# Two activation buffers that begin 12 bytes into a 64-byte line

## The chip, the cores and the metric

The kernel runs on one core of a Trainium2 chip. The metric is the time of one execution on the device in microseconds: 2912.06 us, the median of 3 runs (2911.98 to 2912.39).

## The reference

Two transformer-like blocks are computed one after the other for one sequence of 512 tokens with 1024 features, in float32. Nearly all the work is in dense products of a normalised activation with a weight matrix:

```python
# first block
n = rmsnorm(h, norm_mix_g[l]);  proj = (n @ w_in[l])
y_rwkv = rwkv7_mix(...)         # a recurrent scan over 16 heads, in chunks of 64 tokens
y_attn = dilated_mixture(...)   # 12 heads of windowed attention
merged = sigmoid(gate_r) * (y_rwkv @ p_rwkv) + sigmoid(gate_a) * (y_attn @ p_attn)
h = h + merged @ w_out
h = h + memory_cross_attention(rmsnorm(h), rmsnorm(mem), xa_wq, xa_wkv, xa_wo)
h = h + square(relu(rmsnorm(h) @ ffn_w1)) @ ffn_w2
# second block, two layers
h = rmsnorm_2(x) * (1 + sc1) + sh1
x = x + g1 * token_mix(h, ...)  # fourier_mix and a retention branch, both gated
h = rmsnorm_2(x) * (1 + sc2) + sh2
x = x + g2 * conv_ffn(h, w_up, conv_w, conv_b, w_down)
```

## The kernel before

**Products.** TensorE multiplies float32r operands. To keep float32 accuracy, every operand is split into a high part (rounded to float32r) and a low part (the rest), and each 128 x 128 block of weights gives three matmuls: weight high by activation high, weight high by activation low, weight low by activation high. In `tile` these are L906, L907 and L910. There the weight block is the stationary operand, which is loaded first (PEld in the profile), and a row of the activation with 512 columns (256 for a half tile) is the moving operand, which streams through. Where the output is wanted with tokens on the partitions, the roles are exchanged (L899 to L901): a 128-column piece of the activation is stationary and the weights move.

**Buffers.** Weights come by DMA as units of 128 x 1024 into w_raw (3 slots). ScalarE casts a unit into w_hi (L1862), and GpSimd writes the difference into w_lo (L837, in quarters); w_hi and w_lo have 5 slots. Activations lie in act2 (called A2) and act1 (A1). Each has, on every partition, 2 parts (high, low) of 8 rows of 512 elements of 4 bytes. ScalarE writes a high row (`high`, L1889), VectorE the low row as the difference (`low`, L2600). Smaller buffers follow: act_attn, params, table, tmp, squares, and a large one, arena, which holds nearly all else; arena_r is the same memory as arena seen as float32r, and arena2 is the same memory as act2 seen as float32, used as scratch in the first stages.

**Where they start.** Buffers are laid one behind the other in the order of the program, each rounded up to 32 bytes. From the sizes: w_raw begins at byte 1152 of each partition, w_hi at 13440, w_lo at 33920, act2 at 54400, act1 at 87168, act_attn at 119936, table at 130720, tmp at 137152, squares (and squares_r) at 141248, arena at 148384. Modulo 64 these are 0 for the w and act buffers, tmp and squares, and 32 for table and arena. Rows of act1 and act2 are 2048 bytes apart, so each of them begins at 0 modulo 64. A view in the arena begins wherever the sizes ahead of it put it: `spectrum`, the moving operand of `fourier_tile` (L958 to L960), is at element 16491 of the arena. `folded_tile` (L934 to L936) does the same kind of product from act2. In retention (L1770 to L1772, L1784 to L1786) both operands are data: RK, RQ, RV and RP, whose high parts lie in act_attn, squares_r and act2 and whose low parts lie in the arena.

**Order.** Each engine runs its own list of instructions, fixed when the program is built; they meet at semaphores. The table of tiles (`make_plan`) sets TensorE's order, and four banks of the accumulator are used in turn for them. Nothing in it depends on addresses.

Of the kernel before, what the change touches and what calls it, by code (L numbers as in the profile page):

```python
# [16 lines left out]
P = 128  # L17
F32 = mybir.dt.float32
F32R = mybir.dt.float32r
# [5 lines left out]
S = 512  # L25
M = 256
KT = D // P
# [8 lines left out]
LAYERS = 2  # L36
RING, RAWS = 5, 3
AHEAD = 3
TAIL, W2 = 4, S // 2
BANKS = 4  # L40
ARENA = 20128
# [229 lines left out]
def build_program(nc, plan, ap, out):  # L271
# [19 lines left out]
    with ctx:  # L291
        def sb(name, shape, dt=F32):
            return ctx.enter_context(nc.sbuf_tensor(name, shape, dt))
# [3 lines left out]
        def sem(name):  # L297
            if name not in sems:
                sems[name] = ctx.enter_context(nc.semaphore(name))
            return sems[name]  # L300
# [3 lines left out]
        w_lo = sb("w_lo", [P, RING, UNIT], F32R)  # L304


        with nc.sbuf_tensor("arena2", [P, 2 * KT * S], F32) as arena2:
            pass
        acts = {"A2": sb("act2", [P, 2, KT, S], F32R), "A1": sb("act1", [P, 2, KT, S], F32R)}
        with nc.sbuf_tensor("relu", [P, 2, S], F32) as RELU:  # L310
            pass
        acts["YA"] = sb("act_attn", [P, 2, 2, S], F32R)
# [432 lines left out]
        def half_requests(name):  # L745

            t = stages[CLOSED[name]][1] - 1
            n = TC if name == "final" else TC // 2
            return [(t, n, spare_slots(name)), (t, n, 3)] if name != "out" else [(t, n, 0)] * 2
# [16 lines left out]
        for l in range(LAYERS):  # L766
            if l:
                REQUESTS += half_requests(f"n1_{l}")
            for hd in range(XH):
                before = f"ret_k{l}_{hd + 1}" if hd + 1 < XH else f"ret_g{l}_{hd}"  # L770
                REQUESTS += [(stages[before][1] - 1, TC, AHEAD + (hd + 1 == XH))]
            REQUESTS += half_requests(f"n2_{l}")
# [45 lines left out]
        def _(pool):  # L818
            done = [0]

            def low_weights(end):
                for u in range(done[0], min(end, n_units)):
                    if u in BY_VECTOR:
                        continue
                    k = u % RING
                    pool.wait_ge(sem("w_high" if u else "first_high"), u + 1)
                    if u >= RING:
                        unit_free(pool, u - RING)
                    if u in MIDDLE_UNITS:
                        nc.gpsimd.tensor_tensor(middle_columns(w_lo[:, k, :]), middle_columns(w_raw[:, u % RAWS, :]),  # L830
                                                middle_columns(w_hi[:, k, :].bitcast(F32)), ALU.subtract).then_inc(sem("w_low"), 1)
                        continue
                    for c in range(0, UNIT, UNIT // 4):
                        if u == 0 and c == UNIT // 2:
                            pool.wait_ge(sem("w_high"), 1)
                        cols = slice(c, c + UNIT // 4)
                        ins = nc.gpsimd.tensor_tensor(w_lo[:, k, cols], weights_of(u)[:, cols], w_hi[:, k, cols].bitcast(F32),  # L837
                                                      ALU.subtract)
                        if u < 2 and c < UNIT - UNIT // 4:
                            ins.then_inc(sem("first_low"), 1)  # L840
                    ins.then_inc(sem("w_low"), 1)
                done[0] = max(done[0], min(end, n_units))
# [5 lines left out]
            for r, (t, cols, *ahead) in enumerate(REQUESTS):  # L848
                ahead = ahead[0] if ahead else AHEAD
                low_weights(max(u for u, _, _ in tiles[t]["blocks"]) + 1 + ahead if t is not None else AHEAD)  # L850
                pool.wait_ge(sem("stats_ready"), r + 1)
# [2917 lines left out]
```

## Time and profile before

| | |
|---|---|
| median of 3 runs | 2912.06 us |
| span of the profiled execution | 2909.9 us |
| its own time beside the span | the runs shown lie about 2.2 us above the span |
| PE (matmuls) busy | 2892.3 us, 99% of the span |
| PEld (loads of stationary operands) busy | 2423.8 us, 83% |
| POOL busy | 1584.3 us, 54% |
| DVE busy | 1572.7 us, 54% |
| ACT busy | 1103.5 us, 38% |
| DMA | 322 MB, mean 111 GB/s |

PE is TensorE's matmuls, DVE is VectorE, ACT is ScalarE, POOL is GpSimd. A matmul's duration in the profile runs from its start to its modelled end, and the next one starts before that end, so that durations overlap and a busy share of 99% says only that there is hardly a gap. What a matmul costs in a row of them is the distance from its start to the next one's start, which the list of instructions in order of time gives.

### The profile page before, as it was taken

The page shows a single profiled execution, that of the slowest core. Times are in us where ns is not written, and L with a number is a line of the kernel's source. Part 1 is how long each engine was busy: PE and PEld are TensorE (multiplying, and loading weights), DVE is VectorE, ACT ScalarE, POOL GpSimd, SP SyncE. Part 2 cuts the span into 40 slices and gives each one's busy share as a digit, 9 for nine tenths or more (in the row PEclk, how much of TensorE's full clock was granted, in tenths as well). Part 3 has the DMA queues.
Part 4 walks back from the last instruction along what each step waited for, and adds up shares of the span by engine and source line. Part 5 has one row for each costly group of instructions (what it writes and reads, how often), then busy time and mean ns, then how long its engine had stood idle before and what let it go on. Part 6 is the DMA issues. An engine that isn't in the chain of part 4 may idle for free.

```text
span 2909.9 us, 49401 instructions
## 1 busy us (share of the span) xinstructions
PE 2892.3 (99%) x19658; PEld 2423.8 (83%) x19658; DVE 1572.7 (54%) x2227; ACT 1103.5 (38%) x1673; POOL 1584.3 (54%) x1912
## 2 busy tenths in 40 slices
PE   9999999999999999999999999999999999999998
PEld 7877777788888888888888898888898888988887
DVE  5467877524556666775334265445763441473635
ACT  4454434333443322443433343233443342342323
POOL 6432233355646666677444557565584444565654
PEclk9999999999999999999999999999999999999999
DMA  5211111332426777533222323232333222232232
GB/s 173 94 45 41 42 55 45 97 141 95 130 82 217 252 273 254 179 113 126 85 89 73 95 87 113 87 109 87 106 124 115 77 88 87 87 102 94 94 102 73
DMA packets 92292, 322.21 MB, mean 111 GB/s; under 512 B 10144, under 2 KB 14368, under 8 KB 91808
## 3 DMA queue, kind: packets, MB, share of 16 engines
q1 hardware_dynamic: 84544, 302.39, 31.7%
q10 hardware_dynamic: 7520, 16.67, 1.7%
q8 instruction: 156, 2.56, 0.4%
q14 instruction: 72, 0.59, 0.1%
HBM read 315.09 MB, written 3.93 MB: 110 GB/s over the span
## 4 chain that ended last, share of the span: by engine, by line
PE 98%; issue 1%; DVE 1%; POOL 1%; DMA 0%; ACT 0%; POOLq 0%; SPq 0%; ACTq 0%; DVEq 0%
PE bank L906 25%; PE bank L910 25%; PE bank L907 25%; PE bank L1254 2%; PE bank L899 2%; PE bank L901 2%; PE bank L900 2%; PE bank L1265 2%; PE bank L1273 1%; PE bank L934 1%; PE bank L936 1%; PE bank L935 1%; PE bank L958 1%; PE bank L960 1%; PE bank L1785 1%
## 5 line engine op out<-in xcount | busy, mean ns | idle before, releaser
L837 POOL TENSOR_TENSOR w_lo<-w_raw,w_hi 128x256 fp32r<-128x256 f32 x1736 | 1419.2, 852 | 986.9 <-ACT w_hi L1862 980.5
L906 PE MATMUL bank<-act,w_hi 128*128 128x512 f32 (+1 forms) x3464 | 1312.7, 379 | 4.7 <-POOL w_lo L837 2.6
L910 PE MATMUL bank<-act,w_lo 128*128 128x512 f32 (+1 forms) x3464 | 1292.4, 373 | 0.0
L907 PE MATMUL bank<-act,w_hi 128*128 128x512 f32 (+1 forms) x3464 | 1291.4, 373 | 0.0
L906 PEld LDWEIGHTS bank<-act,w_hi 128*128 128x128 f32 x3464 | 652.9, 188 | 126.1 <-issue 8.3
L910 PEld LDWEIGHTS bank<-act,w_lo 128*128 128x128 f32 x3464 | 652.6, 188 | 115.2
L907 PEld LDWEIGHTS bank<-act,w_hi 128*128 128x128 f32 x3464 | 653.4, 189 | 106.7
L1862 ACT CAST w_hi<-w_raw 128x1024 fp32r<-128x1024 f32 (+1 forms) x438 | 454.4, 1043 | 345.1 <-DMA w_raw<-in_weights 163.6
L1870 ACT ACTIVATE arena<-bank 128x512 f32<-128x512 f32 (+1 forms) x177 | 104.3, 593 | 418.2 <-PE bank L910 401.6
L855 POOL TENSOR_TENSOR stats<-stats,exponent 128x8 f32<-128x8 f32 (+2 forms) x38 | 46.6, 1226 | 302.5 <-DVE stats L2914 150.0
L2600 DVE TENSOR_TENSOR act<-tmp,act 128x512 fp32r<-128x512 f32 (+1 forms) x140 | 121.2, 866 | 77.3 <-ACT act L1889 72.7
L3588 DVE TENSOR_SCALAR arena<-arena,params 128x512 f32<-128x512 f32 x88 | 53.0, 602 | 172.3 <-ACT arena L1870 171.9
L3323 DVE SCALAR_TENSOR_TENSOR arena<-arena,small 128x1024 f32<-128x1024 f32 x93 | 136.5, 1468 | 3.3
L837 POOL TENSOR_TENSOR w_lo<-arena,w_hi 128x256 fp32r<-128x256 f32 x128 | 114.9, 932 | 22.5 <-ACT w_hi L1862 22.5
L1889 ACT CAST act<-tmp 128x512 fp32r<-128x512 f32 (+1 forms) x140 | 84.4, 605 | 112.5 <-DVE tmp L3212 32.0
L2773 DVE SCALAR_TENSOR_TENSOR arena<-bank,small,arena 128x512 f32<-128x512 f32 x48 | 36.1, 751 | 166.9 <-PE bank L910 166.6
L2125 ACT ACTIVATE arena<-bank 128x512 f32<-128x512 f32 (+1 forms) x104 | 64.8, 631 | 114.3 <-PE bank L1273 96.9
L899 PE MATMUL bank<-w_hi,act 128*128 128x512 f32 (+1 forms) x224 | 84.5, 377 | 0.0
L3591 DVE SCALAR_TENSOR_TENSOR arena<-arena,params 128x512 f32<-128x512 f32 x88 | 82.6, 939 | 3.1
L901 PE MATMUL bank<-w_hi,act 128*128 128x512 f32 (+1 forms) x224 | 83.7, 374 | 0.0
L900 PE MATMUL bank<-w_lo,act 128*128 128x512 f32 (+1 forms) x224 | 83.7, 374 | 0.0
L2771 DVE TENSOR_TENSOR arena<-arena,bank 128x512 f32<-128x512 f32 x44 | 30.3, 688 | 89.5 <-PE bank L910 89.2
(359 smaller groups left out, 3087.4 us busy)
## 6 DMA issues: line engine op xcount, KB each, us to landing
w_raw<-in_weights SPq DMA_DIRECT2D x471, 512.0 KB, 3.5
arena<-in_ada SPq DMA_DIRECT2D x96, 512.0 KB, 5.0
arena<-in_strips ACTq DMA_DIRECT2D x8, 448.0 KB, 3.7
arena<-in_x ACTq DMA_DIRECT2D x1, 2048.0 KB, 10.9
y_scratch<-tmp ACTq DMA_DIRECT2D x7, 256.0 KB, 2.0
arena<-y_scratch ACTq DMA_DIRECT2D x1, 1792.0 KB, 8.1
arena<-in_dft ACTq DMA_DIRECT2D x2, 777.5 KB, 4.2
arena<-in_x SPq DMA_DIRECT2D x3, 512.0 KB, 7.4
```

The lines of the kernel that those rows point to most:

```text
L837: ins = nc.gpsimd.tensor_tensor(w_lo[:, k, cols], weights_of(u)[:, cols], w_hi[:, k, cols].bitcast(F32), ALU.subtract)
L899: nc.tensor.matmul(o, xs[0], wh, start=first, stop=False)
L900: nc.tensor.matmul(o, xs[0], wl, start=False, stop=False)
L901: mm = nc.tensor.matmul(o, xs[1], wh, start=False, stop=last)
L906: nc.tensor.matmul(o, wh, xh, start=first, stop=False)
L907: nc.tensor.matmul(o, wh, xl, start=False, stop=False)
L910: mm = nc.tensor.matmul(o, wl, xh, start=False, stop=last)
L1862: nc.scalar.copy(x, y).then_inc(sem("w_high"), 1)
L1870: nc.scalar.activation(dst, banks[bank_of(t)][:, 0:n], func, scale=scale).then_inc(sem(f"bank_free{bank_of(t)}"), 1)
L1889: ins = nc.scalar.copy(o, x) if shift is None else nc.scalar.activation(o, x, ACT.Identity, bias=shift)
L2600: do(V_.tensor_tensor(o, x, h, ALU.subtract), "low_done")
L3323: do(V_.scalar_tensor_tensor(o, w, c_act[:, k:k + 1], o, ALU.mult, ALU.add), "ada_used")
```

## The change

act2, act1 and arena2 get 16 elements (64 bytes) more per partition, and the part that is used begins 3 elements (12 bytes) into them. The rows within a buffer stay 2048 bytes apart. The sub-views are made from the shifted views, so all users follow. act1 begins 64 bytes later than before, everything behind act1 128 bytes later.

```diff
+LINE, LINE_AT = 16, 3
...
-        with nc.sbuf_tensor("arena2", [P, 2 * KT * S], F32) as arena2:
-            pass
-        acts = {"A2": sb("act2", [P, 2, KT, S], F32R), "A1": sb("act1", [P, 2, KT, S], F32R)}
+        with nc.sbuf_tensor("arena2", [P, 2 * KT * S + LINE], F32) as arena2:
+            arena2 = arena2[:, LINE_AT:LINE_AT + 2 * KT * S]
+        acts = {name: sb(buf, [P, 2 * KT * S + LINE], F32R)[:, LINE_AT:LINE_AT + 2 * KT * S].rearrange(
+            "p (a k s) -> p a k s", a=2, s=S) for name, buf in (("A2", "act2"), ("A1", "act1"))}
```

The program has the same 26400 instructions in the same order with the same waits, and the same lengths of their operands; only start addresses differ. Source lines behind the change are 2 higher (L906, L907, L910 become L908, L909, L912).

## Rows read from the trace of the kernel before

**Rows 1.** The page: busy time, and the chain that ended last.
```profile
PE 2892.3 (99%) x19658; PEld 2423.8 (83%) x19658; DVE 1572.7 (54%) x2227; ACT 1103.5 (38%) x1673; POOL 1584.3 (54%) x1912
...
PE 98%; issue 1%; DVE 1%; POOL 1%; DMA 0%; ACT 0%; POOLq 0%; SPq 0%; ACTq 0%; DVEq 0%
```
**Rows 2.** Waits of TensorE: waiter, releaser, us in total, times, longest.
```profile
PE bank L906 <- POOL w_lo L837: 2.6, 2, 2.3
...
PE bank L1312 <- PE bank L1301: 0.2, 1, 0.2
```
**Rows 3.** TensorE's groups by shape: count, busy us and mean ns, idle before.
```profile
L906 PE MATMUL bank<-act,w_hi 128*128 128x512 f32 x2920 | 1156.5, 396 | 2.4 <-POOL w_lo L837 2.3
L910 PE MATMUL bank<-act,w_lo 128*128 128x512 f32 x2920 | 1138.7, 390 | 0.0
L907 PE MATMUL bank<-act,w_hi 128*128 128x512 f32 x2920 | 1137.6, 390 | 0.0
L906 PE MATMUL bank<-act,w_hi 128*128 128x256 f32 x544 | 156.2, 287 | 2.3 <-DVE act L2602 1.0 <-DVE arena L2700 0.8 <-POOL w_lo L837 0.4
...
L899 PE MATMUL bank<-w_hi,act 128*128 128x512 f32 x160 | 62.4, 390 | 0.0
...
L899 PE MATMUL bank<-w_hi,act 128*128 128x384 f32 x64 | 22.0, 344 | 0.0
```
**Rows 4.** In order of time, a long stage: start us, us, instruction.
```profile
1453.28 0.39 PE L910 MATMUL bank<-act,w_lo 128*128 128x512 f32 x1
...
1455.55 0.39 PE L906 MATMUL bank<-act,w_hi 128*128 128x512 f32 x1
```
**Rows 5.** VectorE's groups by shape: two sources on 4-byte words, one shape.
```profile
L2600 DVE TENSOR_TENSOR act<-tmp,act 128x512 fp32r<-128x512 f32 x132 | 116.6, 884 | 76.9 <-ACT act L1889 72.7
...
L2821 DVE TENSOR_TENSOR square_sum<-arena 128x512 f32<-128x512 f32 x27 | 18.9, 701 | 0.9
...
L2600 DVE TENSOR_TENSOR act<-arena,act 128x512 fp32r<-128x512 f32 x16 | 13.7, 857 | 15.3 <-ACT act L1889 15.0
...
L3561 DVE TENSOR_TENSOR arena<-arena 128x512 f32<-128x512 f32 x16 | 11.1, 692 | 0.6
...
L3427 DVE TENSOR_TENSOR arena_r<-bank,arena_r 128x512 fp32r<-128x512 f32 x8 | 5.5, 692 | 16.8 <-ACT arena_r L2385 16.7
```
**Rows 6.** ScalarE's groups by shape: casts.
```profile
L1862 ACT CAST w_hi<-w_raw 128x1024 fp32r<-128x1024 f32 x436 | 453.9, 1047 | 345.1 <-DMA w_raw<-in_weights 163.6 <-PE bank L910 105.3 <-DVE arena L3205 58.7
...
L1862 ACT CAST w_hi<-arena 128x1024 fp32r<-128x1024 f32 x32 | 33.5, 1048 | 32.4 <-DVE arena L3407 19.8 <-DVE arena L3397 12.5
...
L2385 ACT CAST arena_r<-bank 128x512 fp32r<-128x512 f32 x8 | 4.7, 584 | 7.1 <-PE bank L1718 7.1
L2304 ACT CAST act_attn<-bank 128x512 fp32r<-128x512 f32 x8 | 4.3, 590 | 2.8 <-PE bank L1617 2.8
```
**Rows 7.** In order of time, 256 columns from act2 (folded_tile), 14 distances.
```profile
1285.30 0.28 PE L934 MATMUL bank<-act,w_hi 128*128 128x256 f32 x1
...
1286.98 0.28 PE L936 MATMUL bank<-act,w_lo 128*128 128x256 f32 x1
```
**Rows 8.** In order of time, after small matmuls: 7 distances, then 8.
```profile
75.95 0.39 PE L907 MATMUL bank<-act,w_hi 128*128 128x512 f32 x1
...
77.56 0.39 PE L910 MATMUL bank<-act,w_lo 128*128 128x512 f32 x1
...
79.38 0.39 PE L907 MATMUL bank<-act,w_hi 128*128 128x512 f32 x1
```
**Rows 9.** In order of time, retention, 12 distances.
```profile
1418.51 0.40 PE L1784 MATMUL bank<-act,squares_r 128*128 128x512 f32 x1
1418.74 0.40 PE L1785 MATMUL bank<-arena_r,squares_r 128*128 128x512 f32 x1
1418.98 0.40 PE L1786 MATMUL bank<-act,arena_r 128*128 128x512 f32 x1
...
1421.31 0.40 PE L1784 MATMUL bank<-act,squares_r 128*128 128x512 f32 x1
```
**Rows 10.** In order of time, fourier_tile, 18 distances.
```profile
1318.88 0.28 PE L958 MATMUL bank<-arena_r,w_hi 128*128 128x256 f32 x1
...
1321.00 0.28 PE L958 MATMUL bank<-arena_r,w_hi 128*128 128x256 f32 x1
```
**Rows 11.** Stretches: span, busy us and count of each engine, PEclk (granted), DMA.
```profile
1850.00:1950.00 100.00, 100.00 (x443) 82.81 (x442) 51.86 (x64) 34.91 (x49) 67.74 (x80) 1.00 0.32 103
```
**Rows 12.** TensorE's groups by shape between 200 and 560 us.
```profile
L906 PE MATMUL bank<-act,w_hi 128*128 128x512 f32 x209 | 95.6, 457 | 0.0
```

## The prediction

> **What bounds the kernel now.** I read the page's chain of waits first. It gives 98% of the span to TensorE [rows 1], and the list of waits shows under 10 us in which TensorE stood still for another engine, the largest single entry 2.6 us [rows 2]. The reader is to see two things: the end is set by how closely TensorE's matmuls follow each other, and VectorE, ScalarE and GpSimd (54%, 38%, 54% busy) would have to get much slower before they mattered. The second view is the groups by shape [rows 3]: 3 x 2920 matmuls of 512 columns read an activation buffer as the moving operand and a weight slice as the stationary one; 3 x 544 do so with 256 columns; 672 (3 x 160 and 3 x 64) have the roles exchanged. The durations in these rows overlap, so they are not the price. The price is the distance from start to start, read in the third view, the instructions in order of time: in a long stage ten distances take 2.27 us, 227 ns each [rows 4]. 8760 of them make 1989 us, 68% of the span. All depends on whether this 227 moves.
>
> **The change part by part.** No instruction is added, removed or moved; only start addresses differ. w_raw, w_hi and w_lo stay. act2 and act1 each get 64 bytes more, so everything behind them moves by 64 or 128 bytes and keeps its place in a 64-byte line. What changes is every operand in act2, act1 and arena2 (an alias of act2): it begins 12 bytes into a line, an odd 4-byte word.
>
> First, the engines that write and read these buffers. The kernel already has such operands. VectorE's L2821 subtracts two rows of RAW that lie one word apart, so one of them starts on an odd word: 701 ns, against 692 for L3561, whose sources both start 32 bytes into a line. L3427 reads and writes `spectrum`, which lies 12 bytes into a line (148384 + 4 x 16491 bytes; that is 12 modulo 64): 692 ns [rows 5]. ScalarE's cast needs 1048 ns from the odd words of the arena and 1047 from w_raw; its cast into `spectrum` 584, into the aligned act_attn 590 [rows 6]. GpSimd's w_lo touches no moved buffer. So the price here is 0 by the nearest rows. From above I take 9 ns (701 - 692) on the 148 subtractions of L2600 [rows 5] and twice as many others, 4 us, and all of it lies under TensorE, which waits for other engines under 10 us in all. From below it is no gain either. I take 0.
>
> The Trainium skill speaks against the change here: "Vector Engine (DVE) Microarchitecture Reference", section 5.2, says that a port runs at full rate only in runs of adjacent words that start on an 8-byte boundary, and gives 1.30 instead of 1.054 ns per column for pairs on an odd word. By it L2821 and L3427 ought to take over 100 ns more than their neighbours; they don't, so for one long run the trace does not bear it out. Even with it the sum stays, since VectorE is covered.
>
> Second, TensorE's reads. The distance is regular to a degree that tells something: 227 ns for 512 columns, 120 for 256 [rows 4, 7], both 13.3 ns above columns/2.4 GHz; the granted clock is 1.00 in the long stage, the upper of its two levels, 2.4 GHz [rows 11]. But this is a state into which the stream settles. After a few small fp32 matmuls seven distances take 1.61 us, 230 ns each, and the next eight 1.82 us, 227.5 [rows 8]; same operands, same addresses. In retention, 512-column matmuls in which some operands lie 32 bytes into a line (arena) and others 0 (act2, squares_r, act_attn) never settle: twelve distances take 2.80 us, 233.3 ns each, with single ones between 230 and 240 [rows 9]. They are long runs with weights ready, so nothing is waited for. For 256 columns it is the other way round: in fourier_tile the moving operand is `spectrum`, 12 bytes into a line, with the stationary one on a line start from w_hi or w_lo. That is exactly the pairing which the change makes. Eighteen distances (half of 258 columns, half of 256) take 2.12 us, 117.8 ns each, 2.2 below the settled 120 [rows 10]. So 12 bytes do not cost a 256-column matmul anything; they do keep it from the settled rhythm. My reading is that the unsettled rhythm is worth -2 ns at 256 columns and +3 to +7 at 512.
>
> No row shows 512 columns at 12 bytes. The bounds of its price: from below -2.2 ns (rows 10, a gain by instruction), from above +10 (a distance of 237, about the longest that repeats in rows 9). Nearest in length and in steadiness is the retention pattern, +6.6; the settling runs give +3. I take +6.
>
> The sum: of the 8760, some 626 stand in the scan between 200 and 560 us in groups of three to six between small matmuls (209 for L906) [rows 12] and have not settled today, so they cost the same. 8134 x 6 ns = 48.8 us. The 672 with exchanged roles, whose stationary operand now starts at 12 bytes, at the same price: 4.0 us. 1632 of 256 columns x -2.2 ns = -3.6 us. Together +49.2 us. The fp32 matmuls of the scan that read arena2 have their own rhythm and short runs: 0. All of TensorE's time is on the path, so it goes straight to the end: 2909.9 + 49.2 = 2959.1 us of span. The median of the runs shown, 2912.06, lies 2.2 above the span of the profiled execution, which gives 2961.
>
> The Trainium skill, "TensorE: Matmul & The Clock Gate", section "Wait — 56ns, not 53.3ns?", puts back-to-back matmuls at columns/2.4 GHz plus about 2.5 ns, with no word on addresses. By it a 512-column one would follow after 216 ns; the trace has 227, so 11 ns here are something that the page does not know. If they came from two reads that start alike, and the 12 bytes parted them, the sum would be negative: that is case (b) below, driven further.
>
> **The rivals.**
> (a) The rhythm settles again, since all moving operands shift by the same 12 bytes and the weights by none: every matmul meets the next under the same condition, only at another phase. For it: 256 columns settle just as 512 do [rows 7], and settling takes but seven matmuls [rows 8]. Against it: fourier_tile has just such uniform offsets over groups of 24 and does not come to 120. Time: 2912, within 0.2%.
> (b) The other side, faster: what the 12 bytes do at 256 columns they do at 512, because the surplus belongs to the instruction (one weight load) and not to the columns. Price -2.2 ns x (8134 + 672 + 1632) = -23 us: 2889. For it: rows 10 are the only rows with the very pairing. Against it: rows 9, where 512 columns off the settled rhythm are always slower than 227, and rows 8. It decides from the point where the mean distance of L906 falls below 226.7.
> (c) VectorE suffers after all: a quarter more on L2600's 117 us [rows 5] is 29 us, and as much again on the rest. Nearly all of it is hidden under TensorE; if the waits of rows 2 doubled, it would be +10 us, 2922 alone.
> (d) The change doesn't do what it says: act2 and act1 could be placed so that the offset is undone. The kernel's sizes give 54400 + 12 and 87232 + 12, both 12 modulo 64, so no.
>
> **How the numbers follow.** A run of this kernel can be told from another at about 0.2%, 5.8 us. The unsettled rhythm has 0.44 (2961, its own range 2930 to 2998, from +2.5 to +10 ns), the settled one 0.24 (2912), the gain 0.29 (2889, down to 2870), VectorE's part alone 0.03, half of it over the limit. Slower (by over 5.8 us) is thus 0.44 + 0.02 = 0.46, same 0.24 + 0.01 = 0.25, faster 0.29. The range of 8 in 10 takes in the settled case and most of the gain: 2884 to 2995.
>
> **What would show it.** Right: start-to-start distances of the three lines in the long stages near 233 ns and uneven, so that fewer matmuls fall into 100 us (some 430 instead of the 443 of rows 11), while 256-column groups fall to about 118; VectorE's, ScalarE's and GpSimd's means per instruction unchanged; TensorE's waits for others still around 10 us or fewer, clock the same. Wrong: distances flat at 227 (case a), or below it (case b), or waits of TensorE for VectorE or ScalarE of tens of us (case c).

## The result and the profile after

| | before | changed | |
|---|---|---|---|
| median, us | 2912.02 (2911.98 to 2912.39, 4 runs) | 2927.84 (2927.10 to 2928.86, 4 runs) | ratio 1.0054, 95% interval 1.0042 to 1.0067 |
| span of the profiled execution, us | 2909.9 | 2926.8 | +16.9 |

The change makes the kernel slower by 15.8 us; the forecast was +49. The page of the changed kernel gives the busy times, as [rows 1]:

```profile
PE 2906.9 (99%) x19658; PEld 2424.5 (83%) x19658; DVE 1569.3 (54%) x2227; ACT 1101.2 (38%) x1673; POOL 1587.7 (54%) x1912
```

TensorE has 97% of the chain that ended last, where it had 98%. Its busy time grew by 14.6 us; the other three did the same work as before. Its waits (waiter, releaser, us in total, times, longest), against [rows 2]:

```profile
PE bank L908 <- POOL w_lo L839: 4.0, 2, 3.5
```

This wait was 2.6 us, so 1.4 us of the 16.9 may be a wait; nearly all the rest lies between matmuls that wait for nobody. TensorE's groups by shape, against [rows 3] (all lines stand 2 further down):

```profile
L908 PE MATMUL bank<-act,w_hi 128*128 128x512 f32 x2920 | 1162.8, 398 | 3.6 <-POOL w_lo L839 3.5
L909 PE MATMUL bank<-act,w_hi 128*128 128x512 f32 x2920 | 1139.7, 390 | 0.0
L912 PE MATMUL bank<-act,w_lo 128*128 128x512 f32 x2920 | 1138.2, 390 | 0.0
L908 PE MATMUL bank<-act,w_hi 128*128 128x256 f32 x544 | 153.8, 283 | 2.7 <-DVE act L2604 1.1 <-DVE arena L2702 1.0 <-POOL w_lo L839 0.5
```

The group of 256 columns became shorter (287 to 283 ns) and L908's of 512 longer (396 to 398). L909 and L912 have their 390 ns of before, although the stream as a whole is slower: the durations overlap and do not carry the price. It is in the distances from start to start. In order of time, a piece of the long stage of [rows 4]:

```profile
1465.63 0.39 PE L908 MATMUL bank<-act,w_hi 128*128 128x512 f32 x1
...
1469.76 0.39 PE L908 MATMUL bank<-act,w_hi 128*128 128x512 f32 x1
```

Eighteen distances take 4.13 us, 229.4 ns each, where it was 227. The folded tiles of 256 columns, 21 distances, against [rows 7]:

```profile
1292.27 0.28 PE L938 MATMUL bank<-act,w_lo 128*128 128x256 f32 x1
...
1294.73 0.28 PE L938 MATMUL bank<-act,w_lo 128*128 128x256 f32 x1
```

2.46 us, 117.1 ns each, where it was 120. Retention, 12 distances, against [rows 9]:

```profile
1426.61 0.40 PE L1787 MATMUL bank<-arena_r,squares_r 128*128 128x512 f32 x1
...
1429.39 0.39 PE L1787 MATMUL bank<-arena_r,squares_r 128*128 128x512 f32 x1
```

2.78 us, 231.7 ns each (233.3). The stretch of [rows 11] holds 4 matmuls fewer (443 before), at the same clock:

```profile
1850.00:1950.00 100.00, 100.00 (x439) 82.16 (x438) 53.73 (x66) 35.98 (x51) 63.50 (x73) 1.00 0.28 90
```

And the other engines, against [rows 5, 6]:

```profile
L2602 DVE TENSOR_TENSOR act<-tmp,act 128x512 fp32r<-128x512 f32 x132 | 117.7, 892 | 78.5 <-ACT act L1891 74.4
```

L2602, which reads and writes the moved buffers, went from 884 to 892 ns, 1.1 us in all and hidden under TensorE's work; the rest is unchanged (VectorE's L2823 701 to 702 ns, ScalarE's cast L1864 1047 to 1044 ns).

Where the time went, worked out from the start of every matmul of both traces. For each matmul the distance to the next start before the change is subtracted from that after it, and the differences are summed:

| matmuls | count | forecast, us | measured, us | per matmul |
|---|---|---|---|---|
| activations move, 512 columns | 8760 | +48.8 (8134 x 6) | +17.0 | +1.9 ns |
| weights move, 512 and 384 | 672 | +4.0 | +3.6 | +5.3 ns |
| activations move, 256 to 258 (the 1632 and the folded tiles) | 2064 | -3.6 (1632 x -2.2) | -4.7 | -2.3 ns |
| everything else | 8161 | 0 | +1.0 | |
| sum | | +49.2 | +16.8 (of unrounded terms) | |

Of the +1.0 us, 1.2 us is the longer wait for w_lo ahead of the first L908; the others together are 0.2 us shorter.

### The profile page after: what moved, and what is told of

The parts are those of the page before. It is cut to its first block, busy times and chain, and to the rows that moved or that the text cites. A ratio compares the mean times of both kernels' runs of the same rounds, so it can differ in the third digit from the quotient of the medians.

```text
span 2926.8 us, 49401 instructions
## 1 busy us (share of the span) xinstructions
PE 2906.9 (99%) x19658; PEld 2424.5 (83%) x19658; DVE 1569.3 (54%) x2227; ACT 1101.2 (38%) x1673; POOL 1587.7 (54%) x1912
## 4 chain that ended last, share of the span: by engine, by line
PE 97%; POOL 1%; issue 1%; DVE 1%; DMA 0%; ACT 0%; POOLq 0%; SPq 0%; ACTq 0%; DVEq 0%
PE bank L908 25%; PE bank L909 24%; PE bank L912 24%; PE bank L1256 2%; PE bank L901 2%; PE bank L902 2%; PE bank L903 2%; PE bank L1267 2%; PE bank L1275 1%; POOL w_lo L839 1%; PE bank L936 1%; PE bank L938 1%; PE bank L937 1%; PE bank L960 1%; PE bank L962 1%
## 5 line engine op out<-in xcount | busy, mean ns | idle before, releaser
L908 PE MATMUL bank<-act,w_hi 128*128 128x512 f32 (+1 forms) x3464 | 1316.6, 380 | 6.2 <-POOL w_lo L839 4.0
L909 PE MATMUL bank<-act,w_hi 128*128 128x512 f32 (+1 forms) x3464 | 1291.0, 373 | 0.0
L912 PE MATMUL bank<-act,w_lo 128*128 128x512 f32 (+1 forms) x3464 | 1289.4, 372 | 0.0
L908 PEld LDWEIGHTS bank<-act,w_hi 128*128 128x128 f32 x3464 | 650.6, 188 | 131.4 <-issue 8.3
L912 PEld LDWEIGHTS bank<-act,w_lo 128*128 128x128 f32 x3464 | 651.5, 188 | 119.4
L909 PEld LDWEIGHTS bank<-act,w_hi 128*128 128x128 f32 x3464 | 656.7, 190 | 110.9
L1864 ACT CAST w_hi<-w_raw 128x1024 fp32r<-128x1024 f32 (+1 forms) x438 | 452.8, 1040 | 335.9 <-DMA w_raw<-in_weights 147.7
L2602 DVE TENSOR_TENSOR act<-tmp,act 128x512 fp32r<-128x512 f32 (+1 forms) x140 | 122.2, 873 | 78.9 <-ACT act L1891 74.4
L839 POOL TENSOR_TENSOR w_lo<-arena,w_hi 128x256 fp32r<-128x256 f32 x128 | 116.7, 947 | 20.0 <-ACT w_hi L1864 20.0
```

The lines of the kernel that those rows point to most:

```text
L908: nc.tensor.matmul(o, wh, xh, start=first, stop=False)
L909: nc.tensor.matmul(o, wh, xl, start=False, stop=False)
L912: mm = nc.tensor.matmul(o, wl, xh, start=False, stop=last)
L1864: nc.scalar.copy(x, y).then_inc(sem("w_high"), 1)
L2602: do(V_.tensor_tensor(o, x, h, ALU.subtract), "low_done")
```

## Experiments

Theory A was the prediction's: the place within 64 bytes decides, and 12 bytes spoil the rhythm. The padding moves act1 by 64 bytes besides; r1_pad_only was to show that this costs nothing. Below, a word is 4 bytes. The "theory B" in the first recorded text is another than the one formed later: there it is that other engines' accesses disturb TensorE.

**m1_sweep**: TensorE alone, on buffers that begin at the kernel's places modulo 256 bytes (128 bytes behind a multiple), not at its addresses; it computes none of the outputs. Each case has 96 matmuls (shortened):

```
wh, wl = (w[:, st + 5120*q + 1024*slot + P*k : ... + P] for q in range(2))     # stationary, begins at word st
xh, xl = (act[:, mv + KT*S*q + S*k : ... + n] for q in range(2))               # moving, begins at word mv
matmul(o, wh, xh); matmul(o, wh, xl); matmul(o, wl, xh)
```

> TensorE alone: groups of 96 matmuls (four tiles of 8 blocks, weight high by high, high by low, low by high), everything else idle; the output is not the reference's, nearly all work is left out. Moving start swept over 0 to 15 words into a 64-byte line at 512 and 256 columns, stationary start swept over 1 to 15 words at moving 0, both together at 1, 3, 4, 8. Theory A (the reads of TensorE themselves settle or not by the start within a line): 226.7 ns from start to start at moving 0, about 229 at 3 words, about 117 against 120 at 256 columns and 3 words, and some 233 where the stationary operand begins at 3 words; offsets of whole 16-byte units (4, 8, 12 words) like 0 if the unit is 16 bytes, unlike it if it is 64. Theory B (the other engines' accesses to the shifted buffers disturb TensorE): every group at 226.7 and 120, since nothing else runs.

Mean of the last 48 distances of each case, once settled, in ns (512 and 256 columns, stationary operand at 0; last row: stationary moved, moving at 0, 512 columns):

| start, words | 0 | 1 | 2 | 3 | 4 | 5 | 6 | 7 | 8 | 9 | 10 | 11 | 12 | 13 | 14 | 15 |
|---|---|---|---|---|---|---|---|---|---|---|---|---|---|---|---|---|
| 512 | 226.7 | 237.9 | 233.3 | 228.9 | 231.7 | 240.0 | 234.2 | 228.6 | 233.3 | 235.3 | 232.2 | 230.0 | 233.3 | 235.5 | 232.2 | 228.6 |
| 256 | 120.0 | 123.3 | 126.7 | 116.7 | 118.6 | 122.2 | 120.0 | 115.6 | 116.7 | 121.5 | 120.0 | 117.8 | 118.3 | 120.0 | 120.0 | 116.7 |
| stationary | 226.7 | 232.4 | 230.7 | 233.3 | 226.7 | 233.3 | 231.1 | 233.3 | 233.3 | 233.3 | 233.3 | 230.0 | 233.3 | 233.3 | 233.3 | 233.3 |

384 columns took 173.3 at 0 and at 3. Eight moving starts were measured twice at 512 columns and agree to 0.1 ns, except 2 words (233.3 and 232.8). Three of its groups in order of time (start us, us of all 96): 512 columns at 5 words (L76), 256 at 0 (L98) and at 3 (L104):

```profile
156.72 23.25 PE L76 MATMUL bank<-act,w 128*128 128x512 f32 x96
...
410.10 11.75 PE L98 MATMUL bank<-act,w 128*128 128x256 f32 x96
...
447.55 11.45 PE L104 MATMUL bank<-act,w 128*128 128x256 f32 x96
```

So the choice is not between a "settled 227" and an "unsettled 233": each of these places has a settled distance of its own, between 226.7 and 240.0. The changed kernel's 3 words cost 2.2 ns, not 6, and save 3.3 at 256 columns. No other engine was at work, so none is needed for it.

**r1_pad_only**: the padding without the offset (r1 to r3 are shown against the changed kernel).

```diff
-LINE, LINE_AT = 16, 3
+LINE, LINE_AT = 16, 0
```

> The 64 bytes more per buffer stay, the offset is 0. Theory A (the offset within a line does it): as before, 2912 within 3 us, distances flat at 226.7 ns. Rival C (the 64 and 128 bytes by which act1 and all behind it move do it): as the changed kernel, some 2928.

2926.36 us, ratio 1.0051 (1.0038 to 1.0063): nearly all of the loss, with all 12-byte offsets gone. Theory A had it at 2912 and fell here.

**r2_at16**: `LINE_AT = 4`.

> Offset 16 bytes instead of 12. If the unit is 16 bytes or the odd 4-byte word is what disturbs: 2912, distances 226.7. If it is 64 bytes: around 2928, distances 228 to 230 at 512 columns and about 117 at 256.

2946.45 us, ratio 1.0119 (1.0103 to 1.0134). Neither branch had it: not 2912, and more than the 2928 of the 64-byte unit.

**r3_both_12**: as the changed kernel, the weights 12 bytes in as well (W_AT is 3).

```diff
-        w_hi = sb("w_hi", [P, RING, UNIT], F32R)
-        w_lo = sb("w_lo", [P, RING, UNIT], F32R)
+        w_hi, w_lo = (sb(buf, [P, RING * UNIT + LINE], F32R)[:, W_AT:W_AT + RING * UNIT].rearrange(
+            "p (a s) -> p a s", s=UNIT) for buf in ("w_hi", "w_lo"))
```

> w_hi and w_lo begin 12 bytes into a line as well, so that moving and stationary operands start alike again. If only their relative start counts: 2912 and 226.7 flat. If each one's own start counts, the prices add: moving +2.2 ns and stationary +6 ns on 8760 matmuls, some +72 us, 2984; no other engine's work would take longer than 1% more.

2946.4 us, ratio 1.0118 (1.0104 to 1.0132), neither the 2912 nor the 2984 of the two branches. As a test of "both alike" it was badly built: the padding put w_lo 16 words, act2 32 and act1 48 words off w_hi.

**Theory B** was formed on these: what counts is where the two operands start relative to each other, in a period longer than 64 bytes. Before the change w_hi, w_lo, act2 and act1 all lie 128 bytes behind a multiple of 256; in the changed kernel act2 is 3 words and act1 19 words off that.

**m2_far_starts**: TensorE alone with larger offsets.

> TensorE alone, the three matmuls per block of the kernel (high by high, high by low, low by high) from buffers of the same addresses; the moving operand begins 0, 16, 19, 32, 35, 48, 64, 96, 128, 192, 256, 320, 384, 448, 512, 768 and 1024 words (of 4 bytes) further on, then the stationary one, then pairs. The output is not the reference's. Theory A (only the place within 64 bytes counts): every multiple of 16 words gives the 226.7 ns per matmul of 512 columns of offset 0, and 19 and 35 give the 228.9 of 3. Theory B (the starts count relative to each other in a longer period): 16 words give 228 to 233 ns, some larger power of two gives 226.7 again, and from there on all multiples of it do; 19 words (where the changed kernel has act1) give another figure than 3; pairs shifted alike give 226.7.

Five of its groups, moving operand at 0, 16, 3, 19 and 32 words (L148, L150, L152, L154, L156):

```profile
899.33 22.04 PE L148 MATMUL bank<-act,w 128*128 128x512 f32 x96
...
921.79 22.23 PE L150 MATMUL bank<-act,w 128*128 128x512 f32 x96
...
944.44 22.22 PE L152 MATMUL bank<-act,w 128*128 128x512 f32 x96
...
967.09 22.22 PE L154 MATMUL bank<-act,w 128*128 128x512 f32 x96
...
989.73 22.64 PE L156 MATMUL bank<-act,w 128*128 128x512 f32 x96
```

Once settled: 0 gives 226.7; 16, 228.9; 19, 229.2 and 228.9 in its two groups; 32, 232.4 and 233.3; 48, 233.3; 64, 128, 192 up to 1024 words all 226.7 again; 96 is 32 again (232.4). So the period is 64 words, 256 bytes, at the starts measured. The stationary operand moved by 16, 32 and 48 words gives 233.3, 233.3 and 228.9, what the moving one gives for 48, 32 and 16: for these steps of 64 bytes only the difference of the two starts counts. Both moved alike by 16, 32, 64, 128 or 256 words: 226.7. At 256 columns 64, 128 and 256 words give the 120.0 of 0, and 19 words 116.7. But alike by 3 words gave 228.9 in m1_sweep, by 4 words 230.0, by 1 word 237.8, by 8 words 226.7: within 32 bytes the place itself counts too, so "relative" is only half of it.

**r4_behind** and **r5_ahead**: 64 bytes behind act1, and 64 bytes ahead of everything (against the kernel before).

```diff
+        behind = sb("behind", [P, 16])     # r4: behind act1
+        ahead = sb("ahead", [P, 16])       # r5: ahead of w_raw
```

> 64 bytes are put behind act1, so act1, act2 and the weight buffers keep their places and everything behind (act_attn, params, table, tmp, squares, arena) stands 64 bytes further on. Theory B puts the cost on the starts of the matmuls' operands: the time is 2912 as before for all but the few matmuls that read act_attn, table and arena, so 2911 to 2914. Theory C (what the pad-only kernel paid was where the other engines read and write, in step with TensorE's reads): most of the 14 us of that kernel come back, 2920 to 2927.

> 64 bytes are put ahead of the first buffer, so every buffer stands 64 bytes further on and all keep their distances to each other. If the starts count relative to each other (theory B) the time stays 2912, within 1 us. If the absolute place counts (a fixed period of 128 bytes or more in the memory's rows), it is that of the pad-only kernel or more, 2920 to 2930.

2912.46 us (ratio 1.0002, 0.9993 to 1.0011) and 2911.78 (1.0000, 0.9991 to 1.0009). Moving what lies behind act1 by 64 bytes costs nothing, nor does moving everything by 64 bytes.

**r6_slip256** and **r7_twelve_256**: act2's buffer gets 256 bytes of room, so act1 is 256 bytes further on; without an offset, and with 12 bytes in both (shortened, against the changed kernel; the buffers take room and offset from LINES).

```diff
-LINE, LINE_AT = 16, 3
+LINES = {"act2": (64, 0), "act1": (16, 0)}     # r6: (room, offset); r7: offsets 3 and 3
```

> act2 is followed by 256 bytes of room, so act1 begins 256 bytes further on and what is behind it 320, with no offset within a line. Theory B with its period of 256 bytes: act1 stands to the weights as before, so 512 columns keep 226.7 ns and the time is 2912, within 1.5 us. If the period were longer in the whole kernel, or any shift at all counted: 2920 to 2927, as the pad-only kernel.

> act2 begins 12 bytes in, act1 256 + 12 bytes further on than before, so both stand 12 bytes, and nothing else, off the weights in a period of 256; the changed kernel has act1 at 76. TensorE alone showed 228.9 ns for 12 bytes and 229.1 for 76, against 226.7. Theory B: the same time as the changed kernel, 2925 to 2931. If the 64 bytes of the padding were what the changed kernel paid and the 12 bytes were free, it would be 2912 to 2918.

2912.47 us (1.0003, 0.9994 to 1.0012) and 2925.0 (1.0045, 1.0031 to 1.0059; the text on record said 2925 to 2931). 256 bytes are free in the whole kernel, 64 are not; and 12 bytes alone cost what the changed kernel pays but for 3 us. Padding and offset each cost about the same and do not add up, since 19 words are no worse than 3 or 16, and 6264 of the 8760 matmuls read act1, the buffer that the padding moves.

**r8_twenty_256**: as r7, 5 words in place of 3.

> As the twelve_256 kernel with 20 bytes in place of 12: act2 and act1 stand 20 bytes off the weights in a period of 256. TensorE alone showed 240.0 ns at 20 bytes (12: 228.9; 0: 226.7) for 512 columns, 122.2 (116.7; 120.0) for 256. Theory B, that the starts alone set the distance and nothing else in the kernel has a part: of the 2.2 ns that TensorE alone showed at 12 bytes the whole kernel paid 79% (15.35 us over 8760 matmuls of 512 columns), so 13.3 x 8760 x 0.79 = 92 us, 256 columns 2.2 x 1632 = 4 us: 2990 to 3015 us. A rival: outside TensorE alone the other engines' traffic blurs the pattern, and any offset costs the same 13 to 17 us, 2925 to 2930.

3024.0 us, ratio 1.0385 (1.037 to 1.0399): +112, over the range expected. The step that failed is the 79% paid at 12 bytes, carried over to 20 bytes. By the distances of the traces, the 8134 matmuls outside the scan pay 2.0 of 2.2 ns in r7_twelve_256 and 12.7 of 13.3 ns here; the 626 in the scan gave back 0.8 us there and cost 2.5 us here. 13.3 x 8134 = 108, and the measured sum for all 8760 is 105.5 us. Its stretch of [rows 11]:

```profile
1850.00:1950.00 100.00, 100.00 (x418) 80.45 (x417) 35.88 (x47) 27.84 (x37) 54.82 (x69) 1.00 0.29 95
```

Mean distance of the 512-column matmuls between 1750 and 1950 us of every kernel, beside TensorE alone at the same starts (act1 and act2 relative to w_hi, in words modulo 64):

| kernel | us | act2 at | ns | alone | act1 at | ns | alone |
|---|---|---|---|---|---|---|---|
| before, r4, r5, r6 | 2912 | 0 | 226.7 | 226.7 | 0 | 226.7 | 226.7 |
| changed | 2927.84 | 3 | 228.9 | 228.9 | 19 | 229.1 | 228.9, 229.2 |
| r7_twelve_256 | 2925.0 | 3 | 228.9 | 228.9 | 3 | 228.9 | 228.9 |
| r1_pad_only | 2926.36 | 0 | 227.1 | 226.7 | 16 | 228.9 | 228.9 |
| r2_at16 | 2946.45 | 4 | 231.7 | 231.7 | 20 | 231.1 | |
| r8_twenty_256 | 3024.0 | 5 | 240.0 | 240.0 | 5 | 239.9 | 240.0 |

In these kernels the starts give the distance in this stretch, beside working VectorE, ScalarE, GpSimd and DMAs: to 0.1 ns or within the two lone figures in all cells but one, r1's act2 (one cell has no lone figure). r3_both_12 measured 230.5 (act2) and 233.2 (act1) there; no lone run has its starts. In the scan (the 626 between 200 and 560 us) the change took 1.4 ns off each and r8 added 4.0: there the groups of three to six do not pay what the long stages pay.

**m3_pairs**: the low parts moved apart from the high ones, to look for something better.

> TensorE alone, the three matmuls per block as in the kernel; the four parts (weights high and low, activations high and low) are moved apart from each other, at 512, 256, 258 and 384 columns. The output is not the reference's. Theory B (the rhythm hangs on the starts of the two operands relative to each other, in a period of 256 bytes, and a broken relation costs about 1 unit of 6.67 ns per three matmuls): moving only the low activations by 3 or 16 words breaks the relation for one of the three matmuls, so 227.5 to 229; moving the low weights likewise; all four alike is the only way to 226.7 at 512 columns, and no case goes below it. At 256 columns moved starts stay between 115.5 and 126.7 ns, with 7 words among the best and some of 23, 39, 55 near it. A rival: some arrangement at 512 columns is under 226.7, and a better kernel than before can be made of it.

Nothing at 512 columns went below 226.7. Against theory B, w_lo alone may stand 3 or 7 words off and the distance stays 226.7, while the low activations alone, off by 3, bring it to 231.1 and, off by 16, to 232.0. Also against it, the moving operand at 61 words gives 240.0, where the stationary one at 3, the same difference modulo 64, gave 233.3. At 256 columns w_lo at 7 gave 117.8 in place of 120.0. That pointed to a kernel.

**r9_wlo_28**: the kernel before with w_lo 28 bytes in, all others in their places modulo 256. It was to gain on the 256 columns and lose nothing on the 512.

```diff
-        w_lo = sb("w_lo", [P, RING, UNIT], F32R)
+        w_lo = sb("w_lo", [P, RING * UNIT + 64], F32R)[:, 7:7 + RING * UNIT].rearrange("p (r u) -> p r u", u=UNIT)
```

> The kernel before with only w_lo moved: it begins 28 bytes in, and what is behind it stands 256 bytes further on, so w_hi, act1 and act2 keep their places to each other. TensorE alone showed 226.7 ns for 512 columns as before, and 117.8 in place of 120.0 for 256 columns; where the weights move and the activations stand still (480 matmuls of 512 columns) 230.5 in place of 226.7 is the nearest figure. So -2.2 x 1632 = -3.6 us and +3.8 x 480 = +1.8 us: 2910, within 1.5 us; it would be under both kernels if at all by less than 0.2%. If the halves' distances in the kernel don't follow: 2912 to 2914.

2925.11 us (2923.18 to 2927.27), ratio 1.0048 (1.0034 to 1.0061). A miss, and not for the reason named: the 256 columns did fall (-2.4 us over 2064), but the 512 columns rose by 11.6 us. Two stretches tell how. This kernel, then the kernel before, the same 80 us; and this kernel in the stretch of [rows 11]:

```profile
920.00:1000.00 80.00, 80.00 (x347) 64.92 (x346) 52.12 (x46) 22.28 (x27) 51.18 (x58) 1.00 0.74 256
...
1850.00:1950.00 100.00, 100.00 (x443) 82.81 (x442) 54.46 (x67) 36.83 (x52) 66.17 (x76) 1.00 0.30 95
```
```profile
920.00:1000.00 80.00, 80.00 (x355) 66.24 (x354) 54.02 (x48) 23.45 (x29) 54.87 (x60) 1.00 0.76 266
```

At one place of the operands there are two settled rhythms: 226.7 ns in most long stages, and 231.8 in some, over 100 us and more without a change (355 matmuls against 347). TensorE alone had shown only the first, so a lone run at the right starts does not foretell the whole kernel in every case. What throws the stream into the one or the other was not found. No version beat the kernel before.

## Why the prediction was wrong

- *TensorE bounds, and all goes straight to the end*: right. +16.8 us of distances against +16.9 of span.
- *Other engines 0*: right (701 to 702 ns, 1047 to 1044, L2602 +8 ns under cover).
- *12 bytes keep the 512 columns from the settled rhythm, +6 ns*: this step failed. The stream settles again, as rival (a) had it, but at another distance, 228.9 in place of 226.7: +2.2, under the +3 to +7 of my reading and inside its bounds of -2.2 and +10. There is no one "unsettled" price. The retention pattern of [rows 9], which I took for the nearest row, was misread: it does settle. The starts in its trace, to the ns, give 236, 237, 242, 232, 228 and 225 ns, and then the same six again, to 1 ns in all eight passes (so 225 to 242, and not the 230 to 240 that I read). By the sizes of the buffers its moving operand stands 64 bytes before the stationary one, modulo 256, for L1784 and 32 bytes before it for L1785 and L1786, which is 48 and 56 words modulo 64, and TensorE alone gives 233.3 for each of the two (m2_far_starts, m3_pairs). The +6.6 was thus the price of other starts, not of 3 words and not of an unsettled stream. With 2.2 x 8134 = 17.9 in place of 48.8 the same sum gives +18.3 and a time of 2930, where 2927.84 was measured; but that sum has the right size by luck for the part of act1 (next point).
- *Only the 12 bytes change anything, 64 or 128 bytes keep the place in a line*: wrong, and no rival named it. act1's 64 bytes cost the same 2.2 ns by themselves (r1). The time was near to what 12 bytes alone cost (r7, 2925.0) only because 19 words are no worse than 3.
- *8134 and not 8760*: right in the main; r8 shows it best, 105.5 us, near the 108 that 8134 would give and not the 117 of 8760, though 2.5 us of it fall in the scan.
- *672 with the roles exchanged, +6 ns*: near in sum (+5.8 over the 480 of 512 columns, +4.2 over the 384-column ones), and luck in its parts. The 96 whose stationary operand lies in act2, at 3 words, pay +3.0, where TensorE alone has 233.3, +6.6; the 384 in act1, at 19 words, pay +6.5. The place of the stationary operand and not that of the moving one had changed, so the number was no support for the other term.
- *256 columns -2.2 ns*: the number is right (-2.3; TensorE alone 116.7 for 3 words against 120.0), but [rows 10] are not the very pairing that I took them for. `spectrum` is 12 bytes into 64, but 76 bytes into 256, and w_hi is 128, so it stands 51 words off modulo 64 and not 3. That both starts give about 117 ns is luck. For the same reason fourier_tile was no evidence against rival (a): it had not failed to settle, it had its own distance (117.8). Rival (b), which carried this gain to 512 columns, did not come true.
- *The range of the unsettled case*: +10 ns gives 2997 by the same sum, not 2998; nothing hangs on it.

The Trainium skill, "TensorE: Matmul & The Clock Gate", section "Wait — 56ns, not 53.3ns?", has columns/2.4 GHz plus about 2.5 ns for back-to-back matmuls, which is 216 ns for 512 columns, and says nothing of addresses. Here, with float32r operands and a new stationary operand before each matmul, no place came under 226.7, and the place alone made 13.3 ns of difference; the measurement decides.

What stays open: why the distance depends on the starts. One guess is that the read of the moving operand and the load of the next weights get in each other's way. No run separated the two, and a rule by the difference of the starts alone is refuted by the pairs above, so this is not shown.

## What to carry to other kernels

Where TensorE is the bound and its stream is dense, note the start of every matmul operand modulo 256 bytes: equal starts of moving and stationary operands, at the kernel's place or a multiple of 32 bytes from it, gave the best distance for 512 columns here, and a padding of 64 bytes or a new small buffer between them can cost 0.5%, an offset of 20 bytes 3.9%. Pad by 256 bytes or behind the operands. r9_wlo_28 shows that a measurement of TensorE alone can miss: run the whole kernel too. A price taken from a nearby row holds for that row's offsets, and two rows have the same pairing only if their starts agree in the whole period, here 256 bytes and not 64.

## What the runs showed of the hardware that was not expected

- Settled distances at 512 columns between 226.7 and 240.0 ns by the starts alone, at the upper clock (granted 1.00 in the stretches shown); period 256 bytes. At 256 columns 115.6 to 126.7, and not in the same order: 3 words cost 2.2 ns at 512 and save 3.3 at 256; 384 columns gave 173.3 at 0, 3, 7 and 16 words of the moving operand.
- Many of the means are multiples of 6.67 ns (16 cycles of 2.4 GHz) over a short repeat: 226.7 is 34 of them; 228.9 is 103 for three matmuls; 233.3 is 35, 240.0 is 36; at 256 columns 120.0 is 18, 116.7 is 35 for two, 115.6 is 52 for three.
- Two stable rhythms at one set of starts (r9), 226.7 and 231.8 ns, each over whole stages.
